# Experts stage: VectorE takes every subtraction of the second pass, and five u slots follow each head's query slots

## The reference

```python
q = (h @ w_pq).reshape(B, S, PEER_HEADS, 2, PEER_DHALF)
sc = jnp.einsum("bshcd,hcnd->bshcn", q, sub_keys)
s_top, i_top = lax.top_k(sc, PEER_TOPK)
# per head: best 16 of the 16 x 16 sums, softmax -> gate; index = key1 * 128 + key2
a = jax.nn.gelu(jnp.einsum("ced,cd->ce", u_emb[idx], hx), approximate=False)
return jnp.einsum("ce,ced->cd", g * a, v_emb[idx])
```

## Time and profile before

| what | value |
|---|---|
| median of 3 runs | 3267.0 us (3264.32 to 3268.2) |
| the profiled execution | 3261.49 us, span 3259.7 us, mean granted clock 0.991 |
| busy shares of the span | PE 96%, DVE 69%, POOL 39%, ACT 37% |
| first pass (first scores to first matmul of line 1111) | 519.1 to 1285.4 us |
| second pass (line 1111) | 1285.4 to 1885.3 us |

### The profile page before, as it was taken

The page is one execution under the profiler, slowest core; times in us unless marked ns, Lnnn a source line. Parts: engine busy times, 40 slices in busy tenths (PEclk is TensorE's granted clock), DMA queues, the critical chain, the costliest instruction groups (busy, mean ns, idle before and its releaser), DMA issues.

```text
span 3259.7 us, 42914 instructions
## 1 busy us (share of the span) xinstructions
PE 3122.5 (96%) x16170; PEld 2700.5 (83%) x16170; DVE 2252.7 (69%) x3332; ACT 1217.1 (37%) x1818; POOL 1271.7 (39%) x635
## 2 busy tenths in 40 slices
PE   7999999998999998999999999999999999999998
PEld 5877778998989898988888978888588888888886
DVE  7899868998888885998998863204487666522105
ACT  3334543233333333333333353323436564333225
POOL 0010144552344444888888634442020001444432
PEclk9999999999999999999999999999999999999999
DMA  3211133444899999888898722223122222322222
GB/s 126 94 61 46 59 123 123 134 133 155 293 323 338 330 333 345 308 322 318 310 325 314 262 91 97 97 96 126 59 85 72 78 78 78 120 100 97 97 91 91
DMA packets 172859, 548.15 MB, mean 168 GB/s; under 512 B 16825, under 2 KB 41913, under 8 KB 172529
## 3 DMA queue, kind: packets, MB, share of 16 engines
q1 hardware_dynamic: 107968, 380.10, 33.3%
q0 software_dynamic: 36864, 134.23, 12.2%
q10 hardware_dynamic: 27824, 31.08, 2.7%
HBM read 490.60 MB, written 54.55 MB: 167 GB/s over the span
## 4 chain that ended last, share of the span: by engine, by line
PE 61%; DVE 19%; DVEq 9%; DMA 4%; issue 2%; ACTq 2%; ACT 2%; POOL 1%; SPq 0%; POOLq 0%
PE ps L212 41%; PE ps L1111 7%; PE ps L1506 6%; DVEq L1432 4%; DMA experts_back<-experts_dram 3%; DVE conv_out L760 2%; ACTq L1187 2%; DVE gated_lo L1425 1%; DMA ring<-in_stream 1%; PE ps L1086 1%; DVEq L747 1%; ACT slot_parts L196 1%; DVE slot_parts L200 1%; PE ps L1785 1%; DVE h_rows L1439 1%
## 5 line engine op out<-in xcount | busy, mean ns | idle before, releaser
L200 POOL TENSOR_TENSOR slot_parts<-ring,slot_parts 128x1024 fp32r<-128x1024 f32 x362 | 902.6, 2495 | 1332.8 <-ACT slot_parts L196 1332.2
L212 PE MATMUL ps<-h_norm_hi,slot_parts 128*128 128x512 f32 (+1 forms) x4576 | 1361.5, 374 | 54.0 <-DVE slot_parts L200 41.9
L212 PEld LDWEIGHTS ps<-h_norm_hi,slot_parts 128*128 128x128 f32 x4576 | 851.9, 189 | 172.6 <-DVE slot_parts L200 46.2
L212 PE MATMUL ps<-x_low,slot_parts 128*128 128x512 f32 (+1 forms) x2224 | 813.0, 366 | 0.0
L196 ACT ACTIVATE slot_parts<-ring 128x1024 fp32r<-128x1024 f32 x560 | 589.7, 1053 | 484.5 <-DMA ring<-in_stream 315.6
L1111 PE MATMUL ps<-gated_hi,slot_parts 128*128 128x384 f32 x2048 | 549.0, 339 | 36.4 <-DVE gated_lo L1425 24.6
L200 DVE TENSOR_TENSOR slot_parts<-ring,slot_parts 128x1024 fp32r<-128x1024 f32 x198 | 242.8, 1226 | 345.4 <-ACT slot_parts L196 345.1
L212 PEld LDWEIGHTS ps<-x_low,slot_parts 128*128 128x128 f32 x2224 | 422.1, 190 | 49.0
L1111 PEld LDWEIGHTS ps<-gated_hi,slot_parts 128*128 128x128 f32 x2048 | 371.9, 188 | 70.1 <-issue 52.9
L1111 PE MATMUL ps<-gated_lo,slot_parts 128*128 128x384 f32 x1024 | 342.9, 335 | 0.0
L1417 DVE TENSOR_TENSOR gated<-gates_back,experts_back 128x384 f32<-128x384 f32 x128 | 226.3, 1769 | 57.3 <-DMA experts_back<-experts_dram 50.6
(11 more groups left out here) (434 smaller groups left out, 4075.2 us busy)
## 6 DMA issues: line engine op xcount, KB each, us to landing
ring<-in_stream SPq DMA_DIRECT2D x560, 512.0 KB, 3.5
experts_dram<-experts SPq DMA_DIRECT2D x64, 384.0 KB, 5.8
gates_dram<-gates_by_key ACTq DMA_DIRECT2D x24, 1024.0 KB, 18.5
gates_back<-gates_dram SPq DMA_DIRECT2D x32, 768.0 KB, 6.0
experts_back<-experts_dram SPq DMA_DIRECT2D x64, 384.0 KB, 6.0
x_res<-in_xT SPq DMA_DIRECT2D x4, 512.0 KB, 8.2
x_res<-in_xT SPq DMA_DIRECT2D x1, 2048.0 KB, 8.3
v_row<-in_stream,pick_table POOLq DMA_INDIRECT x128, 6.9
```

Of the source, the lines that this page charges most:

```text
L200: e.tensor_tensor(to[:, BUFFER[n], 1, :], ring[:, n % RING, :], to[:, BUFFER[n], 0, :].bitcast(F32), ALU.subtract).then_inc(s_lo, 1)
L212: mm = e.matmul(psum, w2[wv][:, k, :], x2[xv], start=start and v == 0, stop=stop and v == 2)
```

## The change

Two things are changed.

- **Second pass.** POOL's loop is gone: POOL only issues the 128 gathers of v rows, each as soon as its buffer is free. DVE does `slot_lo` of slot i in every iteration, right behind `gated_lo` of i and ahead of the v row.
- **First pass.** `UH` is 5: each head has five u slots behind its two query slots, so 40 u slots are in the part with the heads and 88 behind it, and `TURN` moves from 36 to 44, with the groups (now over u slots 45 to 120) and the dot products (now over 56 to 125) behind it. POOL's share of `slot_lo` grows by 8 slots, DVE's falls by 8. The stream's table of slots is cut to match. The number of all slots, matmuls, groups and gathers is the same.

```diff
-UH = 4
+UH = 5
...
-    ("peer_heads", 48), ("peer_u", 96), ("peer_v", 128),
+    ("peer_heads", (2 + UH) * PH), ("peer_u", NKEY - UH * PH), ("peer_v", 128),
...
-    n_own = n_p + 6 * PH + 5
+    n_own = n_p + (2 + UH) * PH + 5
...
-        for s in range(ROWS_V):
+        for s in range(STEPS):
             v_row(s)
-        e.wait_ge(s_lo, ORDINAL[n_v])
-        for n in range(n_v, n_v + NKEY - 2):
-            slot_lo(e, n)
-            for s in sums_after(n - n_v - 1):
-                if s + ROWS_V < STEPS:
-                    v_row(s + ROWS_V)
         leave(e)
...
                 e.tensor_tensor(G_lo[:, i % GBUF, :], GV[:, i % GBUF, :], G_hi[:, i % GBUF, :].bitcast(F32),
                                 ALU.subtract).then_inc(v_lo, 1)
+                slot_lo(e, n_v + i)
...
-                if i >= NKEY - 2:
-                    e.wait_ge(s_lo, ORDINAL[n_v + i])
-                    slot_lo(e, n_v + i)
```

## The result

The changed kernel takes **3306.2 us** (median of four, 3289.9 to 3323.7); the kernel before, run on the same chip, 3265.7 us (3258.2 to 3268.2). The ratio is 1.0121, with a 95% interval of 1.009 to 1.0151: slower by 40 us, where 23 us less were forecast. The profiled execution is the longest of the four, 3323.7 us, with a mean granted clock of 0.978; the other three had 0.981 to 0.985. A sum of times made on this profile is therefore some 17 us above the median.

A forecast was written before the change was run, and what follows sets the result against it. PE was taken to pace the heads; DVE, contending with POOL, to hold up the second pass; DVE to limit the stretch behind the heads. Second pass -26 and first pass +3 gave -23, about 3243 us from 3267, range 3210 to 3268.

The forecast's parts named there:

- rival (c): Second pass: DVE's busy times are real work, giving 5.45 per slot, +97, about 3365 us; chance 0.02.
- -26 forecast: Second pass: slots go from 4.69 to 4.45 us, 31 us gained, less 5 kept back for its opening and closing sums.
- L = 6.5: Second pass: landing time in us of `experts_back` reads behind `gates_back`, estimated between the median 6.0 and one case's 7.5.
- two slots of PE at 8.34: Second pass: PE's time in us for two slots, during which the read and DVE's following instructions must finish.
- the prediction's own formula: Second pass: every four slots PE loses L - 5.6 where L is above that, plus 0.2 us for spread.
- rival (b): Second pass: the `experts_back` read becomes the replacing wait; no gain at L = 7.6, about 3282 us at 7.9; chance 0.12.
- +3 forecast: First pass: the sum of 24 + 1 - 13 - 9 us, for the heads and the stretch behind them.
- +24 forecast: First-pass heads: seven spacings add 29.6 us, one more slot 4.2, and the 9.1 wait at the transposes falls away.
- -21 forecast: First pass behind the heads: +1 for slots with groups alone, -13 of DVE's work, -9 from shorter waits.
- DVE is the limit, 5.17 against 5.01: First pass behind the heads, before the change: DVE needs 5.17 us per slot, PE 5.01, so DVE paces.
- some 2.2 less in each of four, -9: First pass behind the heads: DVE, now behind, loses 2.2 us less in each wait after ACT's gate DMA issue.
- The bounds of -4 and +15: First-pass term: -4 if PE is the limit with unchanged stalls; +15 without relief in the waits and more late-row waits.

The follow-up runs named there:

- e2: The changed kernel with `UH = 4`, so the second-pass change alone against the kernel before: 3279.0 us, ratio 1.0009 to 1.0057.
- the fills: The changed kernel with 16, 8 or 4 small matmuls by zeros ahead of every fourth second-pass slot: 3339.0, 3303.2 and 3304.6 us.
- e1: The kernel before with `UH = 5`, so the first-pass change alone: 3290.1 us, ratio 1.0048 to 1.011.
- e7: The changed kernel with `UH = 4`, both reads back issued two slots earlier and first-pass gate DMAs spread: 3204.4 us.
- e8: The changed kernel, five u slots per head, with both reads back issued two slots earlier and first-pass gate DMAs spread: 3223.1 us.
- e12: The changed kernel with `gated_lo` and the subtraction of slot j - 1 moved ahead of `gated` of slot j: 3243.1 us.
- e6: The kernel before with ACT's first-pass gate DMAs issued two u slots apart (the last four, one apart): 3240.5 us.

## Why the prediction was wrong

**Contention and DVE's work: right.** `gated` at 0.554, iterations of 3.45 us (starts of `gated` at 1453.11, 1456.56, 1460.01) where 3.46 was said, and no trace of rival (c).

**Second pass, -26 forecast, +13.5 measured in e2. The path was right; two terms of it failed, L = 6.5 and two slots of PE at 8.34.** The forecast was a pass of 575 us (128 x 4.45, and the 5 kept back), e2's profile has 621.7. By the split above, waiting took 63 us and not 40, the lower clock level and the first matmuls behind waits 25 and not 0: 23 and 25 of the 47 missed, and some 22 of the 25 are the clock's. That profile is 23 us above the one of before, where the medians are 13.5 apart, so both parts are smaller in a median run.

- **The read.** "I take L = 6.5" was right for the kernel before: its 32 reads behind `gates_back` took 6.5 us on average. In the changed kernel the same 32 take 7.4, and the 24 landings that stand on the chain in four-fifths of the pass 7.7 (5.7 to 10.4). By the prediction's own formula 7.7 loses 7.7 - 5.6 + 0.2 = 2.3 us per four slots: (4 x 4.17 + 2.3) / 4 = 4.745 per slot, 607 us, and with the 5 kept back 612. That is above the 603 (534 + 69) that the changed kernel's pass would take without the clock, since not every read stood on the chain, and it is no account of the +13.5 by itself. So the step that failed is to take the length of a read from the old kernel over to the new one. The median over all 64 reads did not move (6.0, now 5.8) and could not show it.
- **Why it was longer** stays open. The mean rate in the pass fell (318 to 301 GB/s between 1330 and 1830), but while such a read was under way (from the issue of `gates_back` to the start of `gated`) the DMAs moved 339 GB/s, and 325 before (27 reads each). The Trainium skill (DMA: Bandwidth & Descriptors, Latency and other measured facts) has the access latency of HBM go from 0.2 us on average to 2 at high load; the two pairs, 325 and 6.5, 339 and 7.4, agree in direction. No run changes the load alone, and whether the gathers of v rows, now issued as soon as a buffer is free, have a share was not tried.
- **The clock.** The prediction has PE's two slots on the chain at 8.34 us and PE's clock at 1.00. On the changed kernel's chain 13 such pieces of 23 are 8.6 us and ten are 9.9 to 11.45, on average 9.5. The clock falls behind PE's waits (the fills show that), and as it falls at their end, on the two slots that the next read waits for, the loss goes in full into the pass: some 23 us in that profile, 22 in e2's. The four executions of the changed kernel lie nearly in its order: 3323.7, 3308.8, 3303.6 and 3289.9 us at 0.978, 0.982, 0.981 and 0.985. How much of the 13.5 between the medians is the clock's stays open, for only one execution of each kernel was traced.

It is rival (b), to which I gave 0.12, with its mark too: `gates_back` issued 19.7 us apart on average over the pass (19.4 from 1422.47 to 1539.11), above the 19 named. Its statement that at L = 7.6 no gain is left holds: those 603 us are about the 600 of before. Only the clock makes the changed kernel's pass longer than that, and the rival did not have it.

**First pass, +3 forecast, +24.6 measured in e1.**
- Heads: +24 forecast, +28.2 found (the first u slot behind them at 780.57 before, 808.77 in the changed kernel, 809.42 in e1). The key scores are 33.95 apart, as said. The wait at the transposes did not vanish; it went from 9.10 to 3.18 us. DVE did start 2.0 us after the last scores (762.43 against 760.44), but the last head then took 37.5 us and not the 32.1 that were taken over; two instructions alone are 3.4 of the 5.4 more (`col_hot` 2.89 for 0.69, `gate_sum` 1.38 for 0.19), and why is open.
- Behind the heads: -21 forecast, -5 in e1 (504.8 to 500.0 us). "DVE is the limit, 5.17 against 5.01" was wrong for the kernel before: between the bursts its u slots follow each other by 4.96 us, PE's pace, and 59% of the chain there are PE's u matmuls. In e1 it is 18%, and steps of 5.0 turn to 5.3 and more. All steps but the six longest: 419 to 403 us, -16, near the -12 of the prediction's terms, by luck: DVE as the limit on both sides is not what the trace of before shows.
- The stalls are the step with the wrong sign: "some 2.2 less in each of four, -9". The six longest steps, nearly all behind the bursts, add to 85.6 us before and 97.0 in e1, +11; 83 to 90 in all kernels with bursts and four u slots, 97 to 102 in those with five. The relief was argued from DVE's backlog, but what DVE waits for is ACT, and ACT stands longer in the issue (its six bursts last 71 us before, 84 in e1, 89 in the changed kernel). Why the issue takes longer there was not tried.
- The bounds of -4 and +15 did not hold +24.6. The lower one is not what its terms give either: 24 + 1 + 65 x 5.09 - 73 x 5.01 is -10. Of the 28 lost in the heads 5 came back in e1 (6 from e7 to e8), and only a chance for "the fifth slot is nearly a plain loss" would have covered it.

## What to carry to other kernels

Before work is moved onto an in-order engine, look at which of its waits stands ahead of it and put the work in front of that wait: the order alone is worth 63 us here (e12 against the changed kernel), more than the 40 that the change cost. Price such a wait by the transfers that carry the chain, not by the median of all, and ask at which length the gain is gone: here at 7.6 us, the old kernel's trace said 6.5, and in the new one they took 7.4 to 7.7. A wait of PE of some 2 us can cost more than its length, by the clock behind it. Steps moved to a stretch where PE is the bound cost their full price; they pay it back only if PE is also the bound where they come from.

## What the runs showed of the hardware

- Four DMAs of 1 MB issued in a row from ACT held it for 7 to 18 us; issued one by one, two u slots apart, most of them took 0.37 us (e6: median of 24; the longest 6.8).
- PE's granted clock fell to its lower level behind 13 waits of 1.8 to 4.8 us in the second pass of the changed kernel, at once or up to 1.5 us after PE went on, and not behind four of 2.55 to 2.68. With 0.9 us of each wait filled the clock of the pass was 0.98, with 1.8 us 1.00, with none 0.95.
- The reads of `experts_back` behind `gates_back` took 6.5 us on average before and 7.4 in the changed kernel. The rate over the pass was lower there (301 GB/s for 318), the rate during these reads higher (339 for 325).
